# Features on the partitions from the host: p, the first stage's x and the norm weights of a two-layer trunk

## The reference, cut to what matters

```python
def rms_norm(x, g, eps=1e-6): return x * rsqrt(mean(x*x, -1) + eps) * g
def swiglu(x, w_gu, w_down):
    g, u = split(x @ w_gu, 2); return (silu(g) * u) @ w_down      # 1024 -> 2 x 2816 -> 1024
for i in range(2):
    h = h + 0.5 * rms_norm(swiglu(rms_norm(h, ffn1_pre_g[i]), ffn1_w_gu[i], ffn1_w_down[i]), ffn1_post_g[i])
    u = rms_norm(h, mix_pre_g[i])
    ...                       # two attentions (stick-breaking, differential with diff_subln_g), merged by gates
    h = h + rms_norm(merged @ w_out[i], mix_post_g[i])
    h = h + 0.5 * rms_norm(swiglu(rms_norm(h, ffn2_pre_g[i]), ffn2_w_gu[i], ffn2_w_down[i]), ffn2_post_g[i])
    gate = sigmoid(rms_norm(h, ple_pre_g[i]) @ w_ple_gate[i])
    e = (p[i] @ w_ple_proj[i]) * gate                             # p[i]: 256 tokens x 256
    h = h + rms_norm(e, ple_post_g[i])
```

## Time and profile before

| | |
|---|---|
| median of 3 runs | 1174.02 us (1173.8 to 1174.78) |
| span of the profiled execution, first to last instruction | 1172.6 us |
| difference | 1.4 us |
| busy: TensorE / its weight loads | 1164.0 us (99%) / 983.8 us (84%) |
| busy: VectorE, ScalarE, GpSimd | 850.0 (72%), 721.0 (61%), 53.0 us (5%) |
| moved | 215.37 MB, mean 184 GB/s |

### The profile page before, as it was taken

One profiled execution on the slowest core, in us unless ns is written; L12 is line 12 of the kernel. 1 busy time (PEld: TensorE's weight loads), 2 busy tenths in 40 slices (PEclk: granted clock), 3 DMA queues, 4 the chain that ended last, 5 costly groups with the idle time before them and its releaser, 6 DMA issues.

```text
span 1172.6 us, 17196 instructions
## 1 busy us (share of the span) xinstructions
PE 1164.0 (99%) x6031; PEld 983.8 (84%) x6031; DVE 850.0 (72%) x1290; ACT 721.0 (61%) x1166; POOL 53.0 (5%) x124
## 2 busy tenths in 40 slices
PE   9999999999999999999999999999999999999997
PEld 7888888888888888888888888888888888888886
DVE  6766776977857776676787776678776677677666
ACT  7555556577755755555685655565776566565555
POOL 4000000000000000000100000010000010000002
PEclk9999999999999999999999999999999999999999
DMA  9656564654354555655556565746434446546550
GB/s 296 217 181 212 171 215 164 226 172 152 121 201 146 191 204 185 208 174 211 179 171 198 172 211 179 240 165 198 171 111 179 162 162 215 194 170 209 179 196 37
DMA packets 138655, 215.37 MB, mean 184 GB/s; under 512 B 6958, under 2 KB 97904, under 8 KB 138608
## 3 DMA queue, kind: packets, MB, share of 16 engines
q1 hardware_dynamic: 135808, 208.43, 52.6%
q10 hardware_dynamic: 2576, 6.29, 1.6%
q0 software_dynamic: 224, 0.04, 0.0%
HBM read 213.68 MB, written 1.05 MB: 183 GB/s over the span
## 4 chain that ended last, share of the span: by engine, by line
PE 99%; DMA 0%; DVE 0%; ACT 0%; issue 0%; POOL 0%; POOLq 0%; DVEq 0%; ACTq 0%
PE ps L1673 23%; PE ps L1546 19%; PE ps L1548 18%; PE ps L1547 18%; PE ps L1683 12%; PE ps L1916 3%; PE ps L1593 1%; PE ps L1925 1%; PE ps L1802 1%; PE ps L1817 1%; PE ps L1776 0%; PE ps L1788 0%; DMA raw<-in_w_ple_proj 0%; PE ps L1831 0%; PE ps L1838 0%; PE ps L1803 0%
## 5 line engine op out<-in xcount | busy, mean ns | idle before, releaser
L1106 DVE SCALAR_TENSOR_TENSOR w_lo<-raw,g_layer,w_hi 128x512 fp32r<-128x512 f32 (+1 forms) x504 | 356.3, 767 | 139.2 <-ACT w_hi L644 139.2
L644 ACT ACTIVATE w_hi<-raw,g_layer 128x512 fp32r<-128x512 f32 (+1 forms) x524 | 346.7, 732 | 113.6 <-PE ps L1683 97.0
L1673 PE MATMUL ps<-x_both,w_hi 128*128 128x512 f32 x1152 | 287.7, 392 | 0.0
L1673 PEld LDWEIGHTS ps<-x_both,w_hi 128*128 128x128 f32 x1152 | 209.3, 189 | 39.4 <-issue 0.4
L1546 PE MATMUL ps<-w_hi,x_both 128*128 128x512 f32 x576 | 231.6, 402 | 0.0
L1548 PE MATMUL ps<-w_hi,x_both 128*128 128x512 f32 x576 | 225.0, 391 | 0.0
L1547 PE MATMUL ps<-w_lo,x_both 128*128 128x512 f32 x576 | 224.4, 390 | 0.0
L1103 DVE TENSOR_TENSOR w_lo<-raw,w_hi 128x1024 fp32r<-128x1024 f32 x114 | 134.8, 1221 | 61.3 <-ACT w_hi L641 61.3
L641 ACT ACTIVATE w_hi<-raw 128x1024 fp32r<-128x1024 f32 x114 | 114.7, 1053 | 92.7 <-PE ps L1548 92.5
L1683 PEld LDWEIGHTS ps<-x_both,w_lo 128*128 128x128 f32 x1152 | 152.6, 191 | 8.4
L1683 PE MATMUL ps<-x_both,w_lo 128*128 128x256 f32 x1152 | 156.0, 283 | 0.0
(11 more groups left out here) (230 smaller groups left out, 1041.7 us busy)
## 6 DMA issues: line engine op xcount, KB each, us to landing
raw<-in_ffn_w_gu SPq DMA_DIRECT2D x170, 512.0 KB, 4.6
raw<-in_ffn_w_down SPq DMA_DIRECT2D x88, 512.0 KB, 4.0
raw<-in_w_in SPq DMA_DIRECT2D x80, 512.0 KB, 4.5
raw<-in_w_out SPq DMA_DIRECT2D x16, 512.0 KB, 4.1
raw<-in_w_ple_gate SPq DMA_DIRECT2D x16, 512.0 KB, 4.1
raw<-in_w_branch_sb SPq DMA_DIRECT2D x8, 512.0 KB, 4.1
raw<-in_w_branch_diff SPq DMA_DIRECT2D x8, 512.0 KB, 4.2
raw<-in_ffn_w_gu SPq DMA_DIRECT2D x12, 256.0 KB, 7.8
```

What stands on the lines that cost most here:

```text
L644: last = act.activation(w_hi[:, s, part], raw[:, s, part], ACT.Copy, scale=g_layer[:, g:g + 1])
L1106: last = dve.scalar_tensor_tensor(out=w_lo[:, s, part], in0=raw[:, s, part], scalar=g_layer[:, g:g + 1], in1=whi[:, part], op0=ALU.mult, o ...
L1673: mm = pe.matmul(dst, w_hi[:, s, cols], x_both[:, :, 4 * half + k, :], start=half == 0 and k == 0, stop=stop and k == 3, skip_group_check= ...
```

## The change

The host prepares three more arrays: `x_cols` (x with features on the partitions, 128 x 8 x 256), `p_cols` (the same of p, per layer) and `gain_cols` (the four pre-norm weights and diff_subln_g as 33 columns per layer). The kernel loads them and does no turns for them.

- **p.** `p_raw` (in the place of `p_nat`) gets the two feature halves of p by two DMAs; ScalarE and VectorE split it from there, half k at a time. `turn_p` and its banks go, in both layers. In the first projection the order of TensorE's matmuls becomes feature half by feature half, both token tiles for each piece of weights.
- **x of the first stage.** `x_raw` is two tiles of 512 KB (in the place of `sbq_t` and `sbk_t`, which are free then). The first, for features 0 to 511, is one DMA on ScalarE's queue where x parts 0 and 2 stood. The second is issued by SP between the pieces of unit 1 and those of unit 2. `high_inputs` and `low_inputs` of the first stage read them and wait for the DMA, not for TensorE. The turns of x in the first stage go.
- **Natural x**, still needed for the squares and the residual, is loaded whole: two DMAs of 512 KB on ScalarE's queue, behind the second piece of unit 1 in ScalarE's order.
- **Norm weights.** One DMA by GpSimd into `g_cols`; the turns, VectorE's copies and `start_layer` go, and ScalarE and VectorE read `g_cols` at the layer's column. The factor on diff_subln_g is applied by two instructions of GpSimd, which units 22 and 23 of the mixer wait for.
- **Warm-up**: 17 turns in one row, in place of 13 + 3 and p's four.

The diff, cut to its core:

```diff
-WARM_UP = (13, 3)
+WARM_UP = 17
@@ block.sync
-            for t in range(TT):
-                load_p(t)
+            for k in range(2):
+                sp_.dma_start(p_raw[:, k, :], a["p_cols"][0, :, k, :]).then_inc(p_in[k], 16)
...
             load_pieces(U_PROJ, (1, 3))
-            for u in range(1, PIECED):
-                load_pieces(u)
+            load_pieces(1)
+            sp_.dma_start(x_raw[1][:, :, :], a["x_cols"][:, 4:8, :]).then_inc(xt_in[1], 16)
+            load_pieces(2)
+            load_pieces(3)
@@ block.gpsimd
-            pool.dma_start(g_rows[0:2 * KD, :], a["ffn1_pre_g"].rearrange("l (k p) -> (l k) p", p=P)
-                           ).then_inc(first_g_in, 16)
...
+            pool.dma_start(g_cols[:, :, :], a["gain_cols"][:, :, :]).then_inc(g_in, 16)
...
+            pool.wait_ge(g_in, 16)
+            for i in range(DEPTH):
+                last = pool.tensor_scalar(gain_col(i, G_SUB), gain_col(i, G_SUB), 1.0 - LAM_INIT[i], None, ALU.mult)
+            last.then_inc(sub_scaled, 1)
@@ block.scalar
-            load_x(0)
-            load_x(2)
+            def load_x(t):
+                act.dma_start(h[:, t, :], a["x"][0, t * P:(t + 1) * P, :]).then_inc(h_loaded[t], 16)
+
+            act.dma_start(x_raw[0][:, :, :], a["x_cols"][:, 0:4, :]).then_inc(xt_in[0], 16)
...
+            high_p(0, 0)
             high_piece(U_PROJ, 0)
-            high_p(0, 0, slice(0, P))
             high_piece(U_PROJ, 2)
-            high_p(0, 1, slice(P, SEQ))
+            high_p(0, 1)
             high_piece(U_PROJ, 1)
             high_piece(U_PROJ, 3)
-            load_x(1)
             high_inputs(0, 0, 0, (0,))
-            act.wait_ge(first_g, 1)
+            act.wait_ge(g_in, 16)
             high_piece(1, 0)
             high_piece(1, 1)
-            load_x(3)
+            load_x(0)
+            load_x(1)
             high_piece(1, 2)
             high_inputs(0, 0, 1, (0,))
@@ block.vector
+            low_p(0, 0)
             low_piece(U_PROJ, 0)
-            low_p(0, 0, slice(0, P))
             low_piece(U_PROJ, 2)
-            low_p(0, 1, slice(P, SEQ))
+            low_p(0, 1)
             low_piece(U_PROJ, 1)
             low_piece(U_PROJ, 3)
-            keep_first_gain()
             low_inputs(0, 0, 0, (0,))
+            dve.wait_ge(g_in, 16)
             low_piece(1, 0)
             low_piece(1, 1)
-            keep_gains()
             low_piece(1, 2)
...
-                    start_layer(i + 1)
-                    dve.wait_ge(layer_g, i + 2)
                     low(i + 1, U_PROJ)
@@ block.tensor
-            warm_up(WARM_UP[0])
-            turn_p(0, (0,))
-            warm_up(WARM_UP[1])
-            turn_p(0, (1,))
+            warm_up(WARM_UP).then_inc(units_used, SLOTS)
             first_proj()
...
-                ffn(i, 1, 3, U_FFN2, (lambda: turn_p(i + 1)) if i < LAST else (lambda: None))
+                ffn(i, 1, 3, U_FFN2)
```

More of the change, by code:

```diff
@@ L216, in trunk_kernel @@
         x_split = sem("x_split")
-        h_loaded = [sem(f"h_loaded{n}") for n in range(2 * TT)]
+        h_loaded = [sem(f"h_loaded{t}") for t in range(TT)]
         h_ready = sem("h_ready")
@@ L284, in trunk_kernel @@
         post_in = [sem(f"post_in{s}") for s in range(2)]
-        p_in = [sem(f"p_in{t}") for t in range(TT)]
-        first_g_in = sem("first_g_in")
+        p_in = [sem(f"p_in{k}") for k in range(2)]
+        xt_in = [sem(f"xt_in{n}") for n in range(2)]
         g_in = sem("g_in")
@@ L1479, in _ @@
                 if i < LAST:
-                    low_p(i + 1)
+                    for k in range(2):
+                        low_p(i + 1, k)
                 boundary(i, 2, 4, DOWN_PAIR, lambda k: low_quarter(i, U_GATE + 1, 26, 2, k),
@@ L1645, in turn_last_ht, with pieced @@
                 mm.then_inc(ht_turned, 1)
-            def pieced(u, k, then=None):
+            def pieced(u, k):
                 def wait():
@@ L1745, in ffn @@
                         for t in range(TT):
-                            before = turned_at(0, 0, *{(0, 1): ((1,), (1,)), (1, 0): ((3,), (1,))}.get((s, t), ((), ())))
-                            if t == 0:
-                                before = {k: pieced(u0 + s, k, before.get(k)) for k in range(4)}
+                            before = {k: pieced(u0 + s, k) for k in range(4)} if t == 0 else None
                             mm = first_gate_up(s, t, before)
@@ new lines, in warm_up @@
+                return mm
+            def first_proj():
+                for k in (0, 2, 1, 3):
+                    for t in range(TT):
+                        if k < 2 and t == 0:
+                            pe.wait_ge(p_split, k + 1)
+                        if t == 0 and k < 3:
+                            pe.wait_ge(piece_split, (0, 2, 1).index(k) + 1)
+                        elif t == 0:
+                            begin(0, U_PROJ)
+                        cols, toks = piece(U_PROJ, k), slice(t * P, (t + 1) * P)
+                        mm = exact(bank(E_PAIR[t] + k // 2), p_hi[:, k % 2, toks], p_lo[:, k % 2, toks],
+                                   w_hi[:, slot(U_PROJ), cols], w_lo[:, slot(U_PROJ), cols], k % 2 == 0, k % 2 == 1)
+                        if (t, k) == (0, 3):
+                            mm.then_inc(e_done, 1)
```

189 lines of the change are left out of this document (65 added, 124 removed).

## The result

The changed kernel takes 1175.96 us (median of 21 runs) beside 1174.09 for the kernel before (21 runs, the same chip): ratio 1.0016, interval [1.001, 1.0022]. One of the changed kernel's executions was slow (1654.26 us) and is left out of the ratio. The profiled execution's span is 1174.5 us (1172.6 before). The prediction, 1173.0 with a range to 1175.0, was wrong: the change costs 1.9 us. The loss stays under the 0.2% (2.35 us) that the prediction took for what a measurement tells, but the interval lies above 1, and the prediction had a gain where a loss is.

A forecast was written before the change was run, and what follows sets the result against it. TensorE was taken as the bound (busy 1164.0 of 1172.6 us), with start-up supply limiting the gain: 0.52 there plus 0.44 for layer 1, 0.96 off the span, giving 1171.6; the median lies 1.4 above, 1173.0; range 1171.5 to 1175.0.

The forecast's parts named there:

- rival C: Start-up warm-up: the clock rises some microseconds later than 7.5, giving 1173.0 to 1174.2 us; chance 0.05.
- Bytes: Start-up DMA: 1 MB added; what was issued earlier goes first, each 0.52 MB delays what is behind by 1.4 us.
- The row at 9.00: Earlier trace: a natural x piece issued at 9.00 took 6.5 us to land, read as earlier-issued transfers going first.
- Rival B: Natural x overtakes queued weights: 1174.4 if past unit 3's second piece (first case), 1175.0 if past unit 2's first; chance 0.18.
- (6): Behind unit 3's start: unit 4's last transfer lands at 26.1; its room shrinks to about 0.7 us, stays positive.
- (1): First projection: last weight piece split by 10.35, wanted at 10.8, so no wait; TensorE ends it at about 12.2.
- (2): Unit 1: VectorE has the fourth piece at 14.55, TensorE wants it at 14.2: 0.35 us lost.
- (3): Unit 2: first piece lands at 14.5, then ScalarE's strict order; TensorE waits nearly 1 us, until about 19.05.
- (4): Unit 2's second token tile: fourth part of x stands behind unit 3's second piece (20.4); wait 0.6, end 25.15.
- (5): Unit 3: last piece lands at 23.2, split 24.7; start at 25.15 instead of 25.67, 0.52 us gained of 2.45.
- Layer 1: Layer 0's last FFN: the removed turns of p for layer 1 gain 0.44 us, taken whole.
- the prediction's own sign: Prediction is wrong if more than 0.5 us is lost or won behind 30 us elsewhere than at 550.

The follow-up runs named there:

- the moved square: Changed kernel with natural x issued by SyncE behind unit 3's pieces and the first square moved behind unit 3's last two splits: 1176.53 us.

## Why the prediction was wrong, point by point

- **The clock and the start** (rival C): the PE rows below answer to the earlier trace rows. The first matmul starts at 5.65, and from 5.96 on one starts every 0.23, which was so from 7.50 on. Rival C was false, and the start was better than said (5.93 for the first matmul).

```profile
5.65 0.47 PE L1518 MATMUL ps<-w_hi,p_hi 128*128 128x512 f32 x1 [0.28 <-DVE w_lo L1057]
5.96 0.40 PE L1519 MATMUL ps<-w_lo,p_hi 128*128 128x512 f32 x1
6.19 0.39 PE L1520 MATMUL ps<-w_hi,p_lo 128*128 128x512 f32 x1
```

- **Bytes: the step that failed.** The row at 9.00 was read as priority and was delay. In the changed kernel natural x, issued at 11.13, moves its first packets at 14.9, 3.8 us after its issue. In the kernel before, the piece issued at 9.00 moves its first at 12.8, also 3.8 after. So the window of the earlier trace rows, 8.5 to 10.5, lies within that delay, and its five packets tell nothing of who goes first. From its first packet on a queue takes its turn, packet by packet. The second stretch of the earlier trace rows, 5 to 6 us, shows it in the kernel before, by the lines for its two queues:

```profile
q10 hardware_dynamic: 106, 0.21, 54.7%
q1 hardware_dynamic: 107, 0.19, 49.6%
```

  Rival B had the mechanism at 0.18, its price from 1174.4 to 1175.0; it should have been the forecast. Its first case came out almost to the step: unit 3's second piece at 21.92 (21.8 said), the fourth part of x split at 23.91 (23.8), unit 3 at 26.82 (26.55). What its 1174.4 lacked is the wait in (6) and the mixers.
- **(1) Projection, no wait:** wrong, 1.72 us at 9.92. The second half of the weights comes on SyncE's queue in 2 KB rows, beside the first half of x in 4 KB rows on ScalarE's. Its first piece, the third that TensorE wants, lands at 8.43 instead of 6.62 and is split at 9.80: that is the wait. The last lands at 9.84 instead of 8.97. The step looked at the last piece alone and took its old landing, although ScalarE's queue had got other packets.
- **(2), (3):** a wait of 0.70 where 0.35 stood; unit 2 at 19.27 where 19.05 stood, 0.71 waited where nearly 1 stood. The first piece of unit 2 landed at 14.6 (14.5 said): until here nothing had pushed in front, and the queue's own order was read rightly. ScalarE's strict order was, too.
- **(4) Fourth part of x:** this is where the mis-read law costs most. The structure was right: on ScalarE this part stands behind unit 3's second piece. But that piece lands at 21.92 where 20.4 stood, because both blocks of natural x and not one went past it. At 20.42 it is unit 2's last piece that lands (issued at 8.21, 12.2 to land), and from there on ScalarE makes three splits, each as its piece lands (20.42, 21.17, 21.92). It starts x at 22.58 instead of 21.0, and unit 2 waits twice, 0.82 and 1.44.
- **(5) Unit 3** at 26.82 instead of 25.15: 1.67 off, of which 0.22 stood at unit 2's start and the rest came in (4).
- **(6) Behind:** room was looked for in unit 4's landing and not in what frees the banks of unit 3's second half. That product had no room before (28.39 against 28.44), so each 0.1 us by which ScalarE's fourth part of x is late was on TensorE's path. By the prediction's own 21.0 it would have ended at 28.35, TensorE would have come at 28.15, and 0.2 more would have stood in the sum. The measured wait there is 0.45.
- **Layer 1:** 0.44 said, 0.42 measured. (The start's 0.15 is half of 0.25, so 0.13; it changes nothing.)
- **Elsewhere:** 0.62 us in the mixers, from tiles that the diff moves without naming them. No step looked at the shorter declarations. By the prediction's own sign, more than 0.5 us lost behind 30 us elsewhere than at 550, this alone made it wrong. Without it the changed kernel takes 1175.4, still beyond the range: the supply alone was enough to miss.

## What to carry to other kernels

A transfer on a second queue is priced by packets, not by its place in time: while both queues have work, each gets about as many packets, and the one with the shorter rows gets the fewer bytes, so whatever is not wanted soon should go behind the urgent pieces on the same queue. Before an engine's work is taken out of a start-up stage, follow each strict order in it to its end and write down the room of each wait that is not there yet; a wait of zero length is the next bound. An experiment that moves an instruction can bring such a wait about itself, as the moved square did. And a change of a tile's size moves all tiles declared behind it: hold their places with a pad when two kernels are compared, and try a few places on their own.

## What the runs showed of the hardware

- Two queues with work move about the same number of packets: 88 and 92, 135 and 135, 97 and 95 in a microsecond, with rows of 4 KB against 1 KB, 2 KB against 1 KB, and 4 KB against 1 KB.
- 3.8 us pass from the issue of a transfer on ScalarE's queue to its first packet in this stretch (11.13 to 14.9; 9.00 to 12.8 in the kernel before), where it was 1.3 at the start of the program (0.81 to 2.1). What the time goes into is open.
- A matmul of 128x128 by 512 takes 389 or 392 to 396 ns by where the tile it reads stands in SBUF, to the single float: 16.7 us of 1173 where x_both and ht are in a dear place. The rule behind the places stays open, and in the changed kernel matmuls of x_both, which has not moved, are slower too.
